# Two transformer blocks on one core: the convolution's mean behind two pairs of queries, and the splits, squares and totals of the attention section moved and cut smaller

## The reference, cut to what matters

```python
u = a * jax.nn.sigmoid(g)
u = causal_depthwise_conv(u, conv_w[l], conv_b[l])               # 31 taps, 1024 channels
u = jax.nn.silu(layernorm(u, conv_ln_g[l], conv_ln_b[l]))
q = (rmsnorm(q_lat, q_norm[l]) @ w_uq[l]).reshape(B, S, N_HEADS, QK_HEAD)   # 8 heads of 128 + 64
...
attn = causal_attention(q_full, k_full, v)
mix = jnp.concatenate([rmsnorm(u, conv_out_norm[l]), rmsnorm(attn, attn_out_norm[l])], axis=-1) @ w_out[l]
x = x + rmsnorm(mix, post_mix_norm[l])
```

## Time and profile before

| | |
|---|---|
| runs | 2808.61, 2808.8, 2814.53 us; median 2808.8 |
| profiled execution | 2809.3 us, its span 2807.4 us |
| TensorE busy | 2379.4 us, 85% of the span |
| VectorE busy | 1745.5 us, 62% |
| ScalarE busy | 789.6 us, 28% |
| GpSimd busy | 520.4 us, 19% |
| DMA | 798.92 MB, mean 285 GB/s |

### The profile page before, as it was taken

The page is one execution under the profiler, slowest core; times in us unless marked ns, Lnnn a source line. Parts: engine busy times, 40 slices in busy tenths (PEclk is TensorE's granted clock), DMA queues, the critical chain, the costliest instruction groups (busy, mean ns, idle before and its releaser), DMA issues.

```text
span 2807.4 us, 29432 instructions
## 1 busy us (share of the span) xinstructions
PE 2379.4 (85%) x10942; PEld 1695.0 (60%) x10942; DVE 1745.5 (62%) x2556; ACT 789.6 (28%) x1156; POOL 520.4 (19%) x594
## 2 busy tenths in 40 slices
PE   8997799999999999899899757777777777777776
PEld 8996688888888888799788622222222232222222
DVE  6985547665666566587657985555655555555444
ACT  5433454443444344545431101001100110111010
POOL 0000010000000000100012343333333333333341
PEclk9999899999999999999999989999999999999999
DMA  6542354556555655554588999999999999999997
GB/s 218 177 129 74 93 177 151 193 181 193 184 190 181 193 180 167 161 165 151 167 256 318 416 421 422 422 422 421 421 422 421 421 421 422 421 421 421 422 422 323
DMA packets 339901, 798.92 MB, mean 285 GB/s; under 512 B 23313, under 2 KB 270699, under 8 KB 273771
## 3 DMA queue, kind: packets, MB, share of 16 engines
q0 software_dynamic: 73728, 536.90, 46.0%
q1 hardware_dynamic: 262971, 257.82, 29.0%
q10 hardware_dynamic: 3120, 3.15, 0.3%
HBM read 795.72 MB, written 2.10 MB: 284 GB/s over the span
## 4 chain that ended last, share of the span: by engine, by line
DMA 38%; PE 12%; DVE 7%; issue 1%; POOL 1%; ACT 1%; DVEq 0%; POOLq 0%; PEldq 0%
DMA row<-in_peer_v,expert 31%; DMA row<-in_peer_u,expert 7%; PE pl L808 4%; DVE row L2269 3%; PE pl L1199 3%; PE pl L815 3%; PE pl L811 1%; PE pl L812 1%; POOL row L719 1%; DVE wlo L1745 1%; DMA raw<-in_w_out 0%; PE pl L1128 0%; DVE x_split L1967 0%; DVE tmp L1958 0%; DVE l_xc L2155 0%
## 5 line engine op out<-in xcount | busy, mean ns | idle before, releaser
L1199 PE MATMUL pl<-row,diag 128*128 128x512 f32 x1856 | 862.1, 608 | 337.7 <-DMA row<-in_peer_v,expert 333.3
L2269 DVE CUSTOM_DVE_ANT_0 row<-row,pg 128x2048 f32<-128x2048 f32 x256 | 582.1, 2287 | 458.0 <-DMA row<-in_peer_u,expert 456.7
L1199 PEld LDWEIGHTS pl<-row,diag 128*128 128x128 f32 x1856 | 338.6, 192 | 861.2 <-issue 467.2
L1745 DVE TENSOR_TENSOR wlo<-raw,whi 128x1024 fp32r<-128x1024 f32 (+1 forms) x436 | 517.3, 1208 | 388.1 <-ACT whi L1226 386.5
L1226 ACT ACTIVATE whi<-raw 128x1024 fp32r<-128x1024 f32 (+1 forms) x436 | 444.1, 1039 | 417.0 <-PE pl L815 400.1
L808 PE MATMUL pl<-x_split,whi 128*128 128x512 f32 x1888 | 479.2, 396 | 23.3 <-DVE x_split L1753 12.0
L808 PEld LDWEIGHTS pl<-x_split,whi 128*128 128x128 f32 x1888 | 342.9, 191 | 87.6 <-issue 13.5
L815 PE MATMUL pl<-x_split,wlo 128*128 128x256 f32 x2656 | 373.5, 284 | 3.8 <-DVE wlo L1745 3.8
L815 PEld LDWEIGHTS pl<-x_split,wlo 128*128 128x128 f32 x2656 | 359.1, 192 | 23.0 <-DVE wlo L1745 4.2
L719 POOL DMA_INDIRECT row<-in_peer_u,expert x256 | 240.9, 941 | 635.5 <-PE pl L1199 504.6
L1647 ACT ACTIVATE diag<-ident,dots 128x128 f32<-128x128 f32 x232 | 90.8, 400 | 889.0 <-PE pl L1199 861.0
(11 more groups left out here) (331 smaller groups left out, 1528.8 us busy)
## 6 DMA issues: line engine op xcount, KB each, us to landing
raw<-in_w_in SPq DMA_DIRECT2D x50, 1024.0 KB, 5.4
raw<-in_w_gate SPq DMA_DIRECT2D x44, 1024.0 KB, 5.1
raw<-in_w_up SPq DMA_DIRECT2D x44, 1024.0 KB, 5.1
raw<-in_w_out SPq DMA_DIRECT2D x32, 1024.0 KB, 5.4
raw<-in_w_down SPq DMA_DIRECT2D x32, 1024.0 KB, 5.3
wq<-in_peer_wq SPq DMA_DIRECT2D x13, 1024.0 KB, 10.8
raw<-in_w_down SPq DMA_DIRECT2D x16, 768.0 KB, 4.7
raw<-in_w_ukv SPq DMA_DIRECT2D x4, 1024.0 KB, 5.1
```

Source lines behind the costliest of these rows:

```text
L1199: last = mm(pl[q], diag[:, (at - 1) % 4, :], row[b][:, q * 512:(q + 1) * 512], start=(t == 1 and n == 0 and k == 0), stop=last_row, skip_g ...
L1745: V.tensor_tensor(wlo[:, n % 4, 0:k, :], w[:, :, f, :], whi[:, n % 4, 0:k, :].bitcast(F32), ALU.subtract)\
L2269: V.tensor_tensor_reduce(row[b][:], row[b][:], z_tok[:], 1.0, 0.0, ALU.mult, ALU.add, dots[:, at:at + 1])\
```

## The change

The sum for the convolution's mean moves on TensorE from ahead of head_queries(0, 0) to behind rotate(0), and head_queries(2, 0) moves from pair 0 to right behind it. On VectorE rope(0) goes ahead of the mean. On ScalarE the loop over the pairs is written out: queries_out(1) ahead of the squares for ln; Silu in two halves around prob_out(0) and prob_out(1); squares for conv, and the first weight half of the w_out product, inside pair 1 (they were at the end of pairs 0 and 2); norm_root(conv) from the middle of pair 1 to its end; the input split of tiles 0 to 7 from pair 3 to the end of pair 2, in four steps of two tiles for two steps of four; the squares of the attention output in two steps of four tiles, the first behind pair 1; the second weight half inside pair 3. VectorE follows in kind: rope(1) behind normalise, norm_inverse(conv) and finish(conv) behind normalise(3). TensorE adds up the squares of attention in two parts, inside pair 2 and inside the second half_group. The split of tiles 8 to 15 also goes by two tiles, each scaled and split in turn, and the weights of the third and fourth half_group are split around it, not behind it. A half_group waits for its input by two tiles. `SPLITS` counts on accordingly. No arithmetic is added or left out.

```diff
-            pe.wait_ge(rot_read, 1)
-            pe.wait_ge(conv_step, CONV_K * CT)
-            for t in range(CT):
-                last = mm(pg[2][:, 0:S], ones[:], conv_a[:, t, :], start=(t == 0), stop=(t == CT - 1))
-            last.then_inc(mean_sum, 1)
-
             pe.wait_ge(norm_out, tiles_before(NI["q"] + 1))
             pe.wait_ge(kv_ready, 8)
             head_queries(0, 0)
...
             head_queries(1, 1)
             rotate(0)
+            pe.wait_ge(rot_read, 1)
+            pe.wait_ge(conv_step, CONV_K * CT)
+            for t in range(CT):
+                last = mm(pg[2][:, 0:S], ones[:], conv_a[:, t, :], start=(t == 0), stop=(t == CT - 1))
+            last.then_inc(mean_sum, 1)
+
+            head_queries(2, 0)
             norm_total(NI["ln"], sq_ln)
...
             def between_0():
-                head_queries(2, 0)
                 head_queries(2, 1)
                 rotate(1)
 
             def between_1():
-                norm_total(NI["conv"], conv_a)
                 head_queries(3, 0)
                 rotate(2)
+                norm_total(NI["conv"], conv_a)
+
+            def between_2():
+                head_queries(3, 1)
+                norm_total(NI["attn"], sq_ln, 0, 4)
+
+            def between_3():
+                half_group(PIECE0["out1"], 0, PAIRS[0], arriving="out1", step_of=2)
...
-            half_group(PIECE0["out1"] + 2, 0, PAIRS[1])
-            norm_total(NI["attn"], tmp)
-            half_group(PIECE0["out1"] + 4, 1, PAIRS[0], arriving="out1")
+            half_group(PIECE0["out1"] + 2, 0, PAIRS[1], between=lambda: norm_total(NI["attn"], sq_ln, 4))
+            half_group(PIECE0["out1"] + 4, 1, PAIRS[0], arriving="out1", step_of=2)
             half_group(PIECE0["out1"] + 6, 1, PAIRS[1])
```

ScalarE behind queries_out(0), queries_out(1), squares and root of ln:

```diff
+            exponentials(0)
+            exponentials(1)
+            queries_out(2)
+            act.wait_ge(norm_out, tiles_before(NI["ln"] + 1))
+            conv_out(range(0, 4))
+            prob_out(0)
+            prob_out(1)
+            conv_out(range(4, CT))
+            outputs(0)
+            outputs(1)
+
+            exponentials(2)
+            exponentials(3)
+            act.wait_ge(conv_silu, CT)
+            norm_squares(NI["conv"], mix, conv_a)
+            weights_hi(u, pc, halves=(0,))
+            prob_out(2)
+            prob_out(3)
+            outputs(2)
+            outputs(3)
+            act.wait_ge(o_ready, 4)
+            activation(sq_ln[:, 0:4, :], mix[:, 8:12, :], ACT.Square).then_inc(norm_sq, 1)
+            norm_root(NI["conv"])
+
+            exponentials(4)
+            exponentials(5)
+            queries_out(3)
+            prob_out(4)
+            prob_out(5)
+            outputs(4)
+            outputs(5)
+            act.wait_ge(norm_out, tiles_before(NI["conv"] + 1))
+            for t in range(0, 8, 2):
+                out1_hi(t)
+
+            exponentials(6)
+            exponentials(7)
+            weights_hi(u, pc, halves=(1,))
+            prob_out(6)
+            prob_out(7)
+            outputs(6)
+            outputs(7)
             act.wait_ge(o_ready, HEADS)
-            norm_squares(NI["attn"], mix[:, 8:16, :], tmp)
+            activation(sq_ln[:, 4:8, :], mix[:, 12:16, :], ACT.Square).then_inc(norm_sq, 1)
+            weights_hi(u + 2, pc + 4, halves=(0,))
             norm_root(NI["attn"])
-
-            for t in range(8, DT, 4):
-                act.wait_ge(norm_out, tiles_before(NI["attn"]) + t - 4)
-                copy(xhi[:, t:t + 4, :], mix[:, t:t + 4, :]).then_inc(x_hi, 1)
+            for t in range(8, DT, 2):
+                act.wait_ge(norm_out, tiles_before(NI["attn"]) + t - 6)
+                out1_hi(t)
+            weights_hi(u + 2, pc + 4, halves=(1,))
```

VectorE (rope(0) now stands behind add_taps and ahead of the mean):

```diff
             finish(NI["ln"], conv_a, "conv_ln_g")
-            rope(1)
             normalise(0)
             normalise(1)
+            rope(1)
+
             head_scores(2)
             head_scores(3)
-            norm_inverse(NI["conv"], CONV_CH)
             normalise(2)
             normalise(3)
             rope(2)
+            weights_lo(u, pc, halves=(0,))
+            norm_inverse(NI["conv"], CONV_CH)
             dve.wait_ge(conv_silu, CT)
             finish(NI["conv"], mix, "conv_out_norm")
+
             head_scores(4)
             head_scores(5)
             normalise(4)
             normalise(5)
             rope(3)
-            weights_lo(UNIT0["out1"], PIECE0["out1"], halves=(0,))
+            for t in range(0, 8, 2):
+                out1_lo(t)
+
             head_scores(6)
             head_scores(7)
-            input_lo("out1", mix, (0, 4))
             normalise(6)
             normalise(7)
-            weights_lo(UNIT0["out1"], PIECE0["out1"], halves=(1,))
-            norm_finish(NI["attn"], mix[:, 8:16, :], "attn_out_norm", mix[:, 8:16, :], HEADS * VH)
-            input_lo("out1", mix, (8, 12))
+            weights_lo(u, pc, halves=(1,))
+            weights_lo(u + 2, pc + 4, halves=(0,))
+
+            norm_scale(NI["attn"], HEADS * VH)
+            for t in range(8, DT + 2, 2):
+                if t < DT:
+                    for f in (t, t + 1):
+                        V.scalar_tensor_tensor(mix[:, f, :], mix[:, f, :], col("attn_out_norm", f - 8), rstd[:], ALU.mult, ALU.mult)\
+                            .then_inc(norm_out, 1)
+                if t > 8:
+                    out1_lo(t - 2)
+            weights_lo(u + 2, pc + 4, halves=(1,))
```

More of the change, by code:

```diff
@@ L158 @@
 LATE = ("ffn", "n1", "n2")
-SPLITS = {"in1": 0, "out1": 4, "ffn": 8, "in2": 16, "out2": 24}
+SPLITS = {"in1": 0, "out1": 4, "ffn": 12, "in2": 20, "out2": 28}
 PARAM_TILES = (
@@ L762, in norm_total @@
                     pe.wait_ge(norm_inv, n)
-                for t in range(tiles):
+                for t in range(t0, t1 or tiles):
                     if t % 4 == 0:
@@ L766, in norm_total @@
                     last = mm(pnorm, ones[:], sq[:, t, :], start=(t == 0), stop=(t == tiles - 1))
-                last.then_inc(norm_sum, 1)
+                if (t1 or tiles) == tiles:
+                    last.then_inc(norm_sum, 1)
             def wide_total(name):
@@ L791, in squares, with half_group @@
                     last.then_inc(norm_sum, 1)
-            def half_group(first, half, banks, xs=x_split, k=KU, i=None, step=0, arriving=None, step_of=4, apart=True):
+            def half_group(first, half, banks, xs=x_split, k=KU, i=None, step=0, arriving=None, step_of=4, apart=True, between=None):
                 for f in range(2):
                     n = first + f
+                    if f and between:
+                        between()
                     pe.wait_ge(w_hi, n + 1 if i is None else i * step + (n + 1))
@@ L1415, in _, with conv_out, out1_hi @@
-            weights_hi(UNIT0["out1"], PIECE0["out1"], halves=(1,))
+            def conv_out(tiles):
+                for c in tiles:
+                    activation(mix[:, c, :], conv_a[:, c, :], ACT.Silu, bias=col("conv_ln_b", c)).then_inc(conv_silu, 1)
+            def out1_hi(t):
+                copy(xhi[:, t:t + 2, :], mix[:, t:t + 2, :]).then_inc(x_hi, 1)
+            u, pc = UNIT0["out1"], PIECE0["out1"]
+            exponentials(0)
+            exponentials(1)
+            queries_out(2)
@@ L1843, in _ @@
             V.tensor_tensor(k_pe[:], k_pe[:], k_raw[:], ALU.add).then_inc(roped, 1)
-            add_taps(len(taps))
-            dve.wait_ge(mean_sum, 1)
-            link(V.tensor_scalar(mean_b[:], pg[2][:, 0:S], 1.0 / CONV_CH, None, ALU.mult))
-            for c in range(CT):
-                V.tensor_tensor(conv_a[:, c, :], conv_a[:, c, :], mean_b[:], ALU.subtract).then_inc(centred, 1)
             def rope(n):
@@ L1857, in rope @@
                 V.tensor_tensor(q_pe[:, n, :], q_pe[:, n, :], rot[:, n, :], ALU.add).then_inc(roped, 1)
+            add_taps(len(taps))
+            rope(0)
+            dve.wait_ge(mean_sum, 1)
+            link(V.tensor_scalar(mean_b[:], pg[2][:, 0:S], 1.0 / CONV_CH, None, ALU.mult))
+            for c in range(CT):
+                V.tensor_tensor(conv_a[:, c, :], conv_a[:, c, :], mean_b[:], ALU.subtract).then_inc(centred, 1)
             score = tmp[:, 0:4, :].rearrange("p a b -> p (a b)")
@@ L1892, in finish, with out1_lo @@
                     V.scalar_tensor_tensor(src[:, t, :], src[:, t, :], col(gain, t), rstd[:], ALU.mult, ALU.mult).then_inc(norm_out, 1)
-            rope(0)
+            def out1_lo(t):
+                dve.wait_ge(x_hi, SPLITS["out1"] + t // 2 + 1)
+                V.tensor_tensor(xlo[:, t:t + 2, :], mix[:, t:t + 2, :], xhi[:, t:t + 2, :].bitcast(F32), ALU.subtract)\
+                    .then_inc(x_lo, 1)
+            u, pc = UNIT0["out1"], PIECE0["out1"]
             dve.wait_ge(centred, CT)
```

11 lines of the change are left out of this document (4 added, 7 removed).

## The result

The median of the changed kernel is 2784.12 us (2781.76 to 2786.6, four runs) against 2808.7 (2807.49 to 2814.53, four runs) beside it: ratio 0.9909, 95% interval 0.9891 to 0.9926. It is faster by 24.6 us; 2785 was forecast. The profiled execution is the slowest of the four, 2786.6 us.

What follows compares the result with a forecast made beforehand. The kernel was taken as a string of stages, TensorE's path before 345 us counting fully, with 33.9 us of waits and clock to be had. Terms -12.4 - 0.4 + 0.1 + 3.1 - 9.6 - 6.3 + 1.4 = -24.1 gave 2785 us, range 2780 to 2790.

Steps and rivals of the forecast that it cites:

- Mean behind the queries: TensorE up to the first scores: the mean's sum behind two pairs of queries avoids the 12.3 us wait, -12.4 us.
- Pair 0: First scores to next pair's scores: 13.7 us against 14.1 left after moving queries, set by ScalarE, -0.4 us.
- rival C: Slower: short waits between 252 and 312 us hold the clock at its lower level; 2825 us, chance 0.02.
- Pair 1: Second pair of heads: same products, total and queries swapped, prob_out(2) 0.2 us late at most, +0.1 us.
- Pair 2: Third pair: half the attention total added, scores behind ScalarE's late root and VectorE's finish(conv); 13.9 against 10.8 us, +3.1.
- Pair 3: Last pair to second half_group: earlier splits remove the 5.7 us wait, its clock cost and the 1.4; -9.6 us.
- The last: Second to end of third half_group: 18.1 against 24.4 us, -6.3, plus 1.4 for a possible clock fall.
- Behind that: After the third half_group: pieces and weights arrive before needed, every wait keeps its distance, 0 us.
- The table load: Pair 2's Sqrt and Exp switches: no drain counted; the skill's page would add 1.4 to 2.8 us.
- A: ScalarE and VectorE, in order, hold TensorE up more than counted: gain of 16, 2793 us, chance 0.18.
- B: No gain: time given back in the w_out stage because weights come no faster; 2809 us, chance 0.04.
- My signs: Included first scores 8.5 us earlier, clock 1.00 from 214 to 300 us; wrong if third half_group ends after 319 us.

Runs made afterwards that it cites:

- usual execution: An execution of the changed kernel with only a short clock fall behind pair 0, as in its unedited rerun, median 2784.44 us.
- first profile: Profiled execution of the changed kernel in its first four runs, with a long clock fall behind pair 0: 2786.6 us.
- the mean alone: Kernel before with only the mean's sum behind two pairs of queries, rope(0) and queries_out(1) moved ahead: 2801.64 us, ratio 0.9972.
- the mean with pair 0 reordered: Kernel before with the mean moved, queries_out(2) and prob_out 0 and 1 ahead of Silu, rope(1) behind normalise: 2795.58 us.
- root early: Changed kernel with norm_root(conv) on ScalarE ahead of outputs(2), outputs(3) and the four squares: 2783.25 us, ratio 0.9906.
- late split: Changed kernel with input splits of tiles 0 to 7 back behind exponentials and scores of heads 6 and 7, still by two tiles: 2788.76 us.
- the total in one: Changed kernel with the attention total in one piece of eight tiles inside the second half_group, none in pair 2: 2785.03 us.
- second profile: Profiled execution of the changed kernel run again with no edit: 2783.43 us; median of those four runs 2784.44 us.

## Why the prediction was right, point by point

*Mean behind the queries, -12.4.* 38.2 to 29.6 us with 3.9 moved: -12.5, within 0.1 us.

*Pair 0, -0.4.* It is +0.9 in the usual execution, +0.9 and another 4.6 in pair 1 in the first profile. The waits were counted about rightly (0.9, 0.2 and 1.4 us by the rows, where I had 1.2 ahead of the transposes and the copy of probabilities 1.3 behind them), and so was what ends them, ScalarE's Silu ahead of prob_out. The mis-sized step is the clock: I let none of it fall here, because "a hole of 1.4 us did not do it". That row (317.48) stood behind a half_group at full work. Here three holes come in a row with six short transposes between, and the clock fell every time. My rival C was this mechanism, at the wrong size: it cost 1.0 to 5.6 us, not 40.

And the gain of this part was put into the wrong term. I gave the mean 12.4 us and pair 0's new order 0.4; alone the mean has 6.8, with pair 0 reordered 12.7 to 13.5.

*Pair 1, +0.1*: +0.2 at full clock. *Pair 2, +3.1*: 10.8 to 13.9, exact. Its working has TensorE's own work, with 1.7 us of total, end just ahead of VectorE's chain, and takes the later of the two; so the chain makes the +3.1, and the total is hidden in it (pair 2's transposes begin at the same place without it). The remark that it would be +1.7 without the late finish held: root early has 12.5 against 10.8.

*Pair 3, -9.6*: -9.9. The late split gives 6.4 of it to the place of the input splits; the other 3.5 us (steps of two, the second weight half earlier) had no run of its own. *The last, -6.3 + 1.4*: 24.4 to 19.7, -4.7 in the usual execution. The first high products start at 312.91 behind 2.56 us of wait, and the clock is at 0.50 behind it, as in the value that I took. What this part of the change brings is the earlier start of the scaling:

```profile
305.67 1.89 PE L766 MATMUL pg<-sq_ln,ones 128*128 128x256 f32 x8
...
310.49 1.67 DVE L1973 SCALAR_TENSOR_TENSOR mix<-mix,par,rstd 128x256 f32<-128x256 f32 x4 [0.48 <-ACT rstd L1254]
```

That is 7.7 us behind the start of the second half_group (302.76), where it was 12.0 behind (317.48 to 329.51). With the total in one piece it is 9.3, and the way to the fourth half_group 1.1 us longer than usual. The steps of two have under 1 us of the -4.7. The new places of the weight halves had no run of their own.

*Behind that, 0.* From the start of the fourth half_group to the end of the span it is 2465.6 us before and 2462.6 after; in the other profiles 2462.8 to 2463.6, and 2465.5 in one (the mean alone). In one stage of the second block the granted clock differs between executions. The profiles of before and after at the same work:

```profile
1360.00:1375.00 15.00, 8.69 (x44) 7.24 (x43) 12.33 (x18) 8.65 (x9) 0.00 (x0) 0.68 0.16 53
```

```profile
1340.50:1355.50 15.00, 9.29 (x49) 7.68 (x49) 12.69 (x18) 8.12 (x9) 0.00 (x0) 0.77 0.12 38
```

Since the profile of before is a single one, it is open whether its 2 to 3 us belong to the kernel or the execution. That the mean with pair 0 reordered, which behind pair 0 is the kernel before, has 2463.0 speaks for the execution. So the number of the first profile is put together from a section 18.9 us shorter (109.1 against 128.0), 1.1 us at the start and 3.0 behind it: 23.0 in the span. In the second profile the section alone gives 23.0, and the span is 26.1 shorter. The forecast of 24.1 was for the section alone, and the medians say 24.0 to 24.6: about a microsecond of the agreement is luck.

*The table load.* Ahead of the root the load begins at 278.43, where the squares end (277.36 + 1.06), and the root starts at 279.73. The Trainium skill's drain ("ScalarE: Activation LUTs", "What ACT_TABLE_LOAD costs") does not show here either, and pair 2 came out at 13.9 without it. (From 1.4 to 2.8 us on the forecast are 2786 to 2788 us, not the 2787 to 2788 that I wrote.)

*Rivals.* A in small (ScalarE and VectorE ahead of TensorE in pair 0: 2.6 us with its clock, and 1.3 in pair 2). B did not come: no weight landing stands among TensorE's waits of the section. C as said.

*My signs.* Two of them failed, both through the clock. It was to be 1.00 from 214 to 300 us, and was not. And the prediction was to be wrong if the third half_group ended later than 319 us: in the first profile it ends at 321.84, in the second at 317.79. So one execution of two crosses the line that I had drawn, by the long fall in pair 1, while the time still comes out near the forecast; the line was drawn without a fall. The other signs held: the first scores 8.6 us earlier on the path (38.2 to 29.6), pair 2 near 14 us, VectorE idle for 3.57 us ahead of its finish, no wait for x_split ahead of the first half_group. In the third half_group the first wait is the 2.6 us forecast, and fewer and shorter ones follow than the four of 1 us that I had. The upper end of 2796 us that I set beside rival A has no working: A itself gives 2793.

## What to carry to other kernels

When work is taken from ahead of a wait, ask what it had covered: the mean's move alone gave 6.8 us, with the other engines' queues in pair 0 put right 12.7 to 13.5. In each in-order queue put what the bound engine waits for (probabilities, the root) ahead of what has time (Silu tiles, outputs, squares). Look at the granted clock behind every cluster of short holes, not only behind long ones, and give its fall a range, since neither whether it falls nor for how long could be read off the size of the holes here. Keep work for TensorE in its waits even where it looks free to move away.

## What the runs showed of the hardware

The granted clock fell behind holes of 0.9, 0.2 and 1.4 us with six short transposes between them, in all six profiles that had them. It did not fall in the three profiles where the 1.4 us was gone and the other two holes stood. But the size of the holes does not tell it in advance. Pair 0 of the kernel before has holes of 0.3, 2.2 and 0.2 us around the same transposes, more idle time than these, and keeps its full clock:

```profile
267.56 0.55 PE L981 MATMUL pg<-ident,tmp 128*128 128x128 f32 x3 [2.17 <-DVE tmp L1886]
```

```profile
264.00:270.00 6.00, 3.31 (x16) 2.09 (x16) 2.61 (x9) 2.46 (x7) 0.00 (x0) 1.00 0.75 245
```

With the total in one, a hole of 2.0 us and one of 0.6 behind it in pair 2 brought a fall. What separates these cases is open.

How long the clock stays down is not set by the program alone: about 3 us or about 13 us, worked out from the clocks of the stretches above (0.78 and 0.98, or 0.77 and 0.50), with the same starts to 0.03 us up to there. In the long ones TensorE's rows leave hardly a hole (10.60 of 10.60 us busy at 0.50), so being busy by the rows did not bring the clock back at once. "TensorE: Matmul & The Clock Gate" of the Trainium skill (section "What's actually happening") has two levels of the clock, the lower one as the default, and a moment of change that varies by half a microsecond between runs. The two levels agree with this trace. The variation is larger here, about 10 us at the lower level, or 4.6 us of TensorE's path: the measurement decides.
